# A two-layer hybrid trunk: shifted taps turned later, attention levels in pairs behind whole weight units, other places for the convolution's taps and placements

## The chip, the cores and the metric

The kernel runs on one core of one Trainium2 chip. The metric is the device time of one execution in microseconds (us); lower is better. The kernel before took 1219.56 us, the median of three runs (1218.1 to 1220.88).

## The reference

A decoder trunk over 256 tokens of width 1024, float32 in and out, two layers deep. The part that this change touches is the token mixer:

```python
z = h @ w_in                       # q, k, v, g, gr, ca, cb
gate_logit = gr @ w_gate_up + b_gate
log_a = log_sigmoid(gate_logit) / 16
o = gla_chunked(q * 64**-0.5, k, v, log_a)   # 4 heads, causal, decay exp(cumsum(log_a))
o = rmsnorm(o, gla_norm_w) * silu(g)
u = ca * sigmoid(cb)
u = causal_dwconv(u, conv_w, conv_b)         # 512 channels, 31 taps
u = silu(layernorm(u, cn_w, cn_b))
x = x + concatenate([o, u]) @ w_out
```

Behind the mixer of layer 0 stands a dense SwiGLU (width 2816), behind that of layer 1 a top-2-of-8 mixture of experts of the same width, and at the end an RMSNorm.

## The kernel before

**Weights.** Every weight matrix is cut into units of 128x2048 floats (1 MB). SyncE loads a unit into `raw` (11 slots); ScalarE (ACT) rounds it to a high part `w_hi` (`hi`, L610, 1.9 us); VectorE (DVE) makes the low part `w_lo` (`lo`, L1005, 2.3 us; `lo_half` is half of that). TensorE (PE) multiplies high by high, high by low and low by high. For an input unit these are 48 matmuls of 256 columns (L1728 to L1730 for activations in channel layout, L1762 to L1764 for token layout); `channels("CA1")` is a whole unit, `gates_tile(g, t)` and each half `f` of `channels_unit` are half a unit, 24 matmuls. `b` is the number of a layer's first unit; in layer 0 the units `b+3`, `b+4`, `b+5` are Q, K, V1.

**Attention.** The causal product is taken in nine levels (block sizes 128, 64, ... 1, and the diagonal). `level(n)` on PE (L1982) is a run of small float32 matmuls over 64 rows, 16 records in the trace (8 for level 0). Its input is made by `differences(n)` (DVE), `decays(n)` (ACT, exp) and `decayed(n)` (DVE, L1159, two buffers in turn), and its result is read by ACT for levels 0 to 2 and by `level_read_out(n)` on DVE (L1203) from level 3 on. Two pairs of PSUM banks take the levels in turn, so level n waits for the read-out of level n-2. Behind the levels come `heads()` (L1943 to L1945, the product with v), ACT's `head_squares`, DVE's `head_sums`, ACT's `head_roots`, DVE's `head_gates` (L1178), PE's `turn_heads` (L1955), ACT's `head_hi` (L718), DVE's `head_lo` (L1185).

**Convolution.** Of the four groups of 128 channels, group 0 is done on DVE, one instruction a tap, in two chains `acc` and `acc_odd` (L1123; `conv(k)` on DVE does the next k of 31 taps). Groups 1 to 3 are done on PE (`conv(k)` there, L1917, does the next k of 24 steps, 8 a group), on copies of the input that POOL's DMAs shift (`shifted`), with weights that DVE's `conv_weights` (L1070) expands from the taps `taps_x`. These taps come by DMA as rows in `shift_rows`, and PE turns them (`turn_params`, L2072) into PSUM, from where DVE copies them (L1210). When a group is done, `place(i)` on ACT (L728, four instructions) moves half of it with the bias to `acc`, and `add_ahead(i)` on DVE (L1091, four instructions) adds the other half. `sum_groups(0)` adds groups 0 and 1, and before that `acc_odd` to `acc` (L1103, L1106), `sum_groups(1)` groups 2 and 3. PE takes the layer norm's sums of these (L2052) inside the first output unit (`down_unit`, L1801, six pairs of 512-column matmuls, then the sums of `sum_groups(0)`, three pairs, the sums of `sum_groups(1)`, three pairs), DVE centres (L1349), ACT squares (L832), and PE sums the squares (L2060).

**Order.** Nothing is scheduled by a program. The order of the work on each engine is written out by hand in the function `mixer(l)` of each engine, once for `l == 0` and once for `l == 1` on DVE and ACT, and semaphores tie the engines together.

## Time and profile before

| | us |
|---|---|
| median of three runs | 1219.56 |
| lowest and highest run | 1218.1, 1220.88 |
| profiled execution | 1217.84 |
| its span in the trace | 1216.0 |
| PE busy in the span | 1197.2 |
| DVE busy | 967.0 |
| ACT busy | 783.8 |
| POOL busy | 93.7 |

The profiled execution lies 1.72 us below the median of the runs, and its span 1.84 us below its own time. Layer 0's mixer takes roughly the first 135 us of the span, the dense layer follows until about 320 us, layer 1's mixer until about 440 us, the experts take the rest. A busy PE is not a PE at its peak: each row of PE counts a matmul from issue to its modelled end, so ends overlap the next start. The pace is read from start to start.

### The profile page before, as it was taken

How to read it: one execution, taken by the hardware profiler on the slowest of the kernel's cores; microseconds unless marked ns; L12 is line 12 of the kernel's file. 1: busy time of each engine (PE TensorE's matmuls, PEld its weight loads, DVE VectorE, ACT ScalarE, POOL GpSimd, SP SyncE). 2: the span in 40 equal slices, each digit the busy share in tenths (PEclk: the TensorE clock that was granted, in tenths of full speed). 3: DMA queues.
4: the chain of work that ended last, by engine and by line, in shares of the span. 5: the costliest groups of instructions: out<-in, count | busy, mean ns of one | idle time of the engine just before them, and what ended most of it. 6: DMA issues, size and time to landing. Idle time of an engine off the chain costs nothing.

```text
span 1216.0 us, 16632 instructions
## 1 busy us (share of the span) xinstructions
PE 1197.2 (98%) x6712; PEld 1019.8 (84%) x6712; DVE 967.0 (80%) x890; ACT 783.8 (64%) x693; POOL 93.7 (8%) x160
## 2 busy tenths in 40 slices
PE   8999999999999999999999999999999999999997
PEld 7997999999899788888888888888888888888885
DVE  5988664445668879889979879879879879979987
ACT  5846544334564757677677768658658668767764
POOL 8220000000122000000000000000000000000000
PEclk9999999999999999999999999999999999999998
DMA  8972555655557259999999999999999999999980
GB/s 249 353 243 69 191 174 178 196 180 180 201 177 237 64 190 359 388 362 390 375 366 393 371 373 385 375 371 387 378 384 370 381 382 370 378 384 369 395 328 37
DMA packets 185003, 362.78 MB, mean 298 GB/s; under 512 B 10568, under 2 KB 70746, under 8 KB 184922
## 3 DMA queue, kind: packets, MB, share of 16 engines
q1 hardware_dynamic: 178170, 343.22, 79.3%
q0 software_dynamic: 6736, 18.43, 4.3%
q8 instruction: 56, 0.92, 0.3%
q14 instruction: 25, 0.20, 0.1%
q10 hardware_dynamic: 16, 0.00, 0.0%
HBM read 350.64 MB, written 7.86 MB: 295 GB/s over the span
## 4 chain that ended last, share of the span: by engine, by line
PE 93%; DVE 3%; ACT 2%; SPq 1%; issue 1%; DMA 0%; DVEq 0%; ACTq 0%
PE YB L2199 18%; PE WBS L2178 13%; PE WBS L2180 13%; PE WBS L2179 13%; PE YB L1801 5%; PE WBS L1728 5%; PE WBS L1730 4%; PE WBS L1729 4%; PE YB L2190 2%; PE YB L1782 2%; PE WBS L1762 2%; PE YB L2214 2%; PE WBS L1763 1%; PE WBS L1764 1%; PE YB L1982 1%
## 5 line engine op out<-in xcount | busy, mean ns | idle before, releaser
L1005 DVE TENSOR_TENSOR w_lo<-raw,w_hi 128x2048 fp32r<-128x2048 f32 x319 | 716.2, 2286 | 86.4 <-ACT w_hi L610 86.2
L610 ACT ACTIVATE w_hi<-raw 128x2048 fp32r<-128x2048 f32 x324 | 598.5, 1915 | 13.3 <-DMA raw<-in_w_in 8.1
L2178 PE MATMUL WBS<-w_hi,t_hi 128*128 128x512 f32 x704 | 279.2, 397 | 0.5 <-DVE w_lo L1005 0.5
L2180 PE MATMUL WBS<-w_hi,t_lo 128*128 128x512 f32 x704 | 275.0, 391 | 0.0
L2179 PE MATMUL WBS<-w_lo,t_hi 128*128 128x512 f32 x704 | 274.8, 390 | 0.0
L2178 PEld LDWEIGHTS WBS<-w_hi,t_hi 128*128 128x128 f32 x704 | 132.3, 188 | 29.1 <-issue 1.5
L2180 PEld LDWEIGHTS WBS<-w_hi,t_lo 128*128 128x128 f32 x704 | 132.3, 188 | 28.6
L2179 PEld LDWEIGHTS WBS<-w_lo,t_hi 128*128 128x128 f32 x704 | 132.5, 188 | 26.0
L1728 PE MATMUL WBS<-t_hi,w_lo 128*128 128x256 f32 x448 | 127.8, 285 | 0.0
L1729 PE MATMUL WBS<-t_hi,w_hi 128*128 128x256 f32 x448 | 126.9, 283 | 0.0
L1730 PE MATMUL WBS<-t_lo,w_hi 128*128 128x256 f32 x448 | 126.8, 283 | 0.0
L956 ACT ACTIVATE eT_hi<-YB 128x512 fp32r<-128x512 f32 (+1 forms) x48 | 27.0, 563 | 148.3 <-PE YB L2214 148.3
L2199 PE MATMUL YB<-w_hi,eT_hi 128*128 128x512 f32 x320 | 101.6, 399 | 0.3 <-DVE eT_lo L1652 0.3
L2199 PE MATMUL YB<-w_hi,eT_lo 128*128 128x512 f32 x320 | 100.7, 396 | 0.0
L2199 PE MATMUL YB<-w_lo,eT_hi 128*128 128x512 f32 x320 | 100.1, 394 | 0.0
L1728 PEld LDWEIGHTS WBS<-t_hi,w_lo 128*128 128x128 f32 x448 | 85.9, 192 | 1.5 <-issue 0.7
L1729 PEld LDWEIGHTS WBS<-t_hi,w_hi 128*128 128x128 f32 x448 | 86.0, 192 | 0.4
L1730 PEld LDWEIGHTS WBS<-t_lo,w_hi 128*128 128x128 f32 x448 | 86.0, 192 | 0.0
L2199 PEld LDWEIGHTS YB<-w_lo,eT_hi 128*128 128x128 f32 x320 | 60.1, 188 | 14.9
L2199 PEld LDWEIGHTS YB<-w_hi,eT_lo 128*128 128x128 f32 x320 | 60.1, 188 | 14.1
L2199 PEld LDWEIGHTS YB<-w_hi,eT_hi 128*128 128x128 f32 x320 | 59.4, 188 | 14.4 <-issue 0.7
L962 ACT ACTIVATE eg<-WBS 128x512 f32<-128x512 f32 (+1 forms) x48 | 26.9, 560 | 65.6 <-PE WBS L2180 65.6
(320 smaller groups left out, 1389.2 us busy)
## 6 DMA issues: line engine op xcount, KB each, us to landing
raw<-in_we_down SPq DMA_DIRECT2D x88, 1024.0 KB, 7.1
raw<-in_we_gate SPq DMA_DIRECT2D x80, 1024.0 KB, 6.8
raw<-in_we_up SPq DMA_DIRECT2D x80, 1024.0 KB, 6.6
raw<-in_w_in SPq DMA_DIRECT2D x19, 1024.0 KB, 6.5
raw<-in_wd_gate SPq DMA_DIRECT2D x11, 1024.0 KB, 5.4
raw<-in_wd_up SPq DMA_DIRECT2D x11, 1024.0 KB, 5.3
raw<-in_wd_down SPq DMA_DIRECT2D x11, 1024.0 KB, 5.0
raw<-in_w_out SPq DMA_DIRECT2D x8, 1024.0 KB, 9.5
```

Of the source, the lines that this page charges most:

```text
L610: act.activation(w_hi[:, hi_slot(n, item), :], raw[slot][:], ACT.Copy).then_inc(hi_ready, 1)
L956: act.activation(eT_hi[:, 0:w, :], YB[:, 3, 0:P * w].rearrange("p (f t) -> p f t", f=w), ACT.Copy).then_inc(eT_hi_ready, 1)
L962: act.activation(eg[:, 0:w], WB[c % 2][:, 0:w], ACT.Silu).then_inc(egate_ready, 1)
L1005: dve.tensor_tensor(w_lo[slot][:], raw[slot][:], w_hi[:, hi_slot(n, item), :].bitcast(F32), ALU.subtract).then_inc(lo_ready, 1)
L1728: pe.matmul(dst, lo[:, k, cols], t_hi[:, k, :], start=(k == 0), stop=False)
L1729: pe.matmul(dst, hi[:, k, cols], t_hi[:, k, :], start=False, stop=False)
L1730: ins = pe.matmul(dst, hi[:, k, cols], t_lo[:, k, :], start=False, stop=(k == KD - 1))
L1801: ins = pe.matmul(YB[:, 2 * t + half, :], a[:, k0 + k, tok], w[:, k, HALF * half:HALF * (half + 1)], start=(first and k == 0 and s), stop= ...
L2178: pe.matmul(bank, xs_hi[:, k0 + k, :], hi[:, k, :], start=start, stop=False)
L2179: pe.matmul(bank, xs_hi[:, k0 + k, :], lo[:, k, :], start=False, stop=False)
L2180: ins = pe.matmul(bank, xs_lo[:, k0 + k, :], hi[:, k, :], start=False, stop=stop)
L2199: ins = pe.matmul(YB[:, half, :], a[:, f, :], w[:, k, HALF * half:HALF * (half + 1)], start=(first and s), stop=(last and e))
```

## The change

- **The shifted taps.** `turn_params` no longer waits for `shift_rows` nor turns them. A new `turn_shift_rows` on PE turns them into PSUM bank YB 3 between the units CB0 and Q of layer 0; a new `shifted_taps` on DVE copies them to `taps_x` between `lo(b + 4)` and `conv_input(0)`; K, which is multiplied into the same bank, waits for that copy. `shift_rows` now lies in the memory of `acc_odd`, and its old place stays as filler. The buffer `idle` grows from 40 to 48 floats a partition, which moves all that is allocated behind it by 32 bytes.
- **The levels.** Before, levels 2 to 6 each stood behind or inside one half unit, and 7 and 8 together behind the last. After, levels 2 and 3 stand behind all of CA1, 4 and 5 behind both halves of G0, 6 and 7 behind both halves of G1; then come two steps of the convolution, level 8, and the other six of the group.
- **The placements.** On ACT `place(1)` moves ahead of `head_hi()`. On DVE `add_ahead(1)` moves ahead of the two `head_lo`.
- **DVE's taps.** In layer 0 seven are new behind `lo(b + 6)`, 12 instead of 14 stand ahead of `conv_input(1)`, four behind the `conv_weights` instead of three before them and one behind, none behind `head_gates` or `head_lo`. In layer 1 the 14 become 12, and five stand behind `head_lo` instead of two before and one behind. `level_read_out(7)` and `(8)` now stand ahead of the last two `conv_weights`.

```diff
@@ memory
-        idle = sb("idle", [P, 40])
+        idle = sb("idle", [P, 48])
-        shift_rows = sc("shift_rows", [P, L, P])
-        sc("beside_cu", [P, 2880 - L * P])
+        sc("beside_cu", [P, 2880])
         acc_odd = sm("acc_odd", [P, T])
+        shift_rows = acc_odd[:].rearrange("p (l c) -> p l c", l=L)
@@ ACT, mixer(l), both layers
                     head_roots()
+                    place(1)
                     head_hi()
-                    place(1)
                     place(2)
@@ DVE
+            def shifted_taps():
+
+                dve.wait_ge(shift_turned, 1)
+                dve.wait_ge(gr_done, 1)
+                dve.tensor_copy(taps_x.rearrange("p l q b -> p (l q b)"), YB[:, 3, 0:L * QS * 24]).then_inc(taps_x_ready, 1)
+
             def conv_weights(l, i):
 
                 if l == 0 and i == 0:
                     dve.wait_ge(ident4_ready, 1)
+                    dve.wait_ge(taps_x_ready, 1)
...
                 if l == 0:
-                    dve.wait_ge(turned_rows, 2 + L)
-                    dve.wait_ge(gr_done, 1)
-                    dve.tensor_copy(taps_x.rearrange("p l q b -> p (l q b)"), YB[:, 2, 0:L * QS * 24])
+                    dve.wait_ge(turned_rows, 2)
@@ DVE, mixer(0)
                     lo(b + 4)
+                    shifted_taps()
                     conv_input(0)
                     lo(b + 5)
                     conv(6)
                     lo(b + 6)
+                    conv(7)
                     decayed(0)
...
-                    conv(14)
+                    conv(12)
                     conv_input(1)
...
                     level_read_out(6)
-                    conv(3)
+                    level_read_out(7)
+                    level_read_out(8)
                     conv_weights(0, 1)
                     conv_weights(0, 2)
-                    level_read_out(7)
-                    level_read_out(8)
-                    conv(1)
+                    conv(4)
                     add_ahead(0)
                     head_sums(0)
                     head_sums(1)
                     head_gates()
-                    conv(2)
+                    add_ahead(1)
                     head_lo(0)
                     head_lo(1)
-                    conv(3)
-                    add_ahead(1)
                     sum_groups(0)
@@ DVE, mixer(1)
-                    conv(14)
+                    conv(12)
...
                     level_read_out(6)
+                    level_read_out(7)
+                    level_read_out(8)
                     conv_weights(1, 1)
                     conv_weights(1, 2)
-                    level_read_out(7)
-                    level_read_out(8)
                     add_ahead(0)
...
                     head_gates()
-                    conv(2)
+                    add_ahead(1)
                     head_lo(0)
                     head_lo(1)
-                    conv(1)
-                    add_ahead(1)
+                    conv(5)
                     sum_groups(0)
@@ PE, mixer(l)
                 if l == 0:
                     pe.wait_ge(params_ready, 1)
+                    turn_shift_rows()
                 channels("Q")
+                if l == 0:
+                    pe.wait_ge(taps_x_ready, 1)
                 channels("K")
...
-                channels("CA1", between=lambda: level(2))
-                channels("CB1", between=lambda: level(3))
+                channels("CA1")
+                level(2)
+                level(3)
+                channels("CB1")
                 gates_tile(0, 0)
+                gates_tile(0, 1)
                 level(4)
-                gates_tile(0, 1)
                 level(5)
                 gates_tile(1, 0)
+                gates_tile(1, 1)
                 level(6)
-                gates_tile(1, 1)
                 level(7)
+                conv(2)
                 level(8)
-                conv(8)
+                conv(6)
                 heads()
@@ PE, turn_params
-                pe.wait_ge(shift_rows_ready, 16 * L * QS * 2)
...
-                for rows, n in ((shift_rows[:, 0, :], 24 * QS), (shift_rows[:, 1, :], 24 * QS), (tap_rows[:], L * TAPS * 2), (pv_rows[:], L * NPV + KD)):
+                for rows, n in ((tap_rows[:], L * TAPS * 2), (pv_rows[:], L * NPV + KD)):
...
+            def turn_shift_rows():
+
+                pe.wait_ge(shift_rows_ready, 16 * L * QS * 2)
+                n = 24 * QS
+                for l in range(L):
+                    ins = pe.transpose(YB[:, 3, n * l:n * (l + 1)], shift_rows[0:n, l, :], ident[0:n, 0:n])
+                ins.then_inc(shift_turned, 1)
```

## Rows read from the trace of the kernel before

**Rows 1.** The page: the span, and the chain that ended last, by engine.
```profile
span 1216.0 us, 16632 instructions
...
PE 93%; DVE 3%; ACT 2%; SPq 1%; issue 1%; DMA 0%; DVEq 0%; ACTq 0%
```

**Rows 2.** Windows, the experts: stretch, length, busy PE, PEld, DVE, ACT, POOL, PEclk, DMA, GB/s.
```profile
470.00:1216.00 746.00, 736.69 (x3331) 602.60 (x3329) 648.52 (x473) 524.83 (x387) 26.92 (x19) 1.00 0.98 362
```

**Rows 3.** Timeline of PE, levels 4 and 5: start, duration (us), engine, line, operation.
```profile
71.31 1.11 PE L1982 MATMUL YB<-qkE 64*128 64x64 f32 x16
...
75.42 1.11 PE L1982 MATMUL YB<-lnw 64*128 64x64 f32 x16
```

**Rows 4.** Timeline of PE, end of G1, levels 7 and 8, the convolution before and after the heads.
```profile
83.30 0.28 PE L1763 MATMUL WBS<-w_lo,t_hi 128*128 128x256 f32 x1
83.42 0.28 PE L1764 MATMUL WBS<-w_hi,t_lo 128*128 128x256 f32 x1
83.63 1.11 PE L1982 MATMUL YB<-lnw 64*128 64x64 f32 x16
84.57 1.11 PE L1982 MATMUL YB<-qk 64*128 64x128 f32 x16
85.61 3.67 PE L1917 MATMUL WBS<-shifted,shift_w 128*64 128x256 f32 x32
...
92.09 4.97 PE L1917 MATMUL WBS<-shifted,t_mem 128*64 128x256 f32 x44
```

**Rows 5.** Timeline of PE, level 1 (behind level 0) and the first matmuls of CA1.
```profile
53.33 1.01 PE L1982 MATMUL YB<-lnw 64*128 64x64 f32 x16
54.27 0.39 PE L1728 MATMUL WBS<-t_hi,w_lo 128*128 128x256 f32 x1
54.49 0.28 PE L1729 MATMUL WBS<-t_hi,w_hi 128*128 128x256 f32 x1
```

**Rows 6.** Timeline of PE, the turned rows at the start, and the next matmul.
```profile
19.08 0.39 PE L2072 MATMUL YB<-ident,shift_rows 96*128 96x96 f32 x2 [2.81 <-DMA pv_rows<-in_ln_w]
19.30 0.27 PE L2072 MATMUL YB<-ident,tap_rows 124*128 124x124 f32 x1
```

**Rows 7.** Timeline of DVE, layer 0, two places ahead of the levels' products.
```profile
47.83 0.69 DVE L1159 TENSOR_TENSOR qkE<-qk,Difs 128x512 f32<-128x512 f32 x1 [2.81 <-ACT qk L693]
...
73.24 0.68 DVE L1159 TENSOR_TENSOR lnw<-qk,Difs 128x512 f32<-128x512 f32 x1
```

**Rows 8.** Timeline of PE, layer 0, the layer norm's sums inside the first output unit.
```profile
104.68 0.71 PE L2052 MATMUL WBS<-shifted,ones 128*128 128x128 f32 x4 [0.79 <-DVE shifted L1106]
...
106.88 0.71 PE L2052 MATMUL WBS<-shifted,ones 128*128 128x128 f32 x4
...
109.38 1.83 PE L2060 MATMUL WBS<-shifted,ones 128*128 128x128 f32 x14 [0.39 <-ACT shifted L832]
```

**Rows 9.** Timeline of DVE, layer 0, from behind the last `head_lo` to the half unit ahead of the centring.
```profile
100.70 0.47 DVE L1123 SCALAR_TENSOR_TENSOR acc<-cu,taps,acc 128x256 f32<-128x256 f32 x1
101.09 0.48 DVE L1123 SCALAR_TENSOR_TENSOR acc_odd<-cu,taps,acc_odd 128x256 f32<-128x256 f32 x1
...
102.00 1.71 DVE L1091 TENSOR_TENSOR acc<-acc,WBS 32x240 f32<-32x240 f32 x4
...
106.74 1.22 DVE L1012 TENSOR_TENSOR w_lo<-raw,w_hi 128x1024 fp32r<-128x1024 f32 x1
```

**Rows 10.** Timeline of ACT, layer 0: `head_hi`, then `place(1)` and `place(2)`.
```profile
98.66 1.27 ACT L718 ACTIVATE t_hi<-WBS,pv 128x512 fp32r<-128x512 f32 x2 [3.62 <-PE WBS L1955]
99.81 3.89 ACT L728 ACTIVATE acc<-WBS,pv 32x256 f32<-32x256 f32 x8
```

**Rows 11.** Timeline, layer 1: DVE's `sum_groups(0)`, PE's sums and sums of squares.
```profile
409.25 0.43 DVE L1106 TENSOR_TENSOR shifted<-acc 128x256 f32<-128x256 f32 x1
...
409.74 0.71 PE L2052 MATMUL WBS<-shifted,ones 128*128 128x128 f32 x4
...
414.43 1.83 PE L2060 MATMUL WBS<-shifted,ones 128*128 128x128 f32 x14 [0.39 <-ACT shifted L832]
```

More of the change, by code:

```diff
@@ L271, in trunk @@
         cgate_ready, cu_ready, pads_ready = (sem(s) for s in ("cgate_ready", "cu_ready", "pads_ready"))
+        shift_turned, taps_x_ready = sem("shift_turned"), sem("taps_x_ready")
         shift_rows_ready, shift_pads, conv_grouped, odd_added = (sem(s) for s in (
@@ L479, in _ @@
             step(pool.memset(ones[:], 1.0))
-            step(pool.memset(shift_rows[:], 0.0))
+            step(pool.memset(shift_rows, 0.0))
             for l in range(L):
@@ L823, in mixer @@
                     head_roots()
+                    place(1)
                     head_hi()
-                    place(1)
                     place(2)
@@ L1207, in mixer @@
                 if l == 0:
-                    dve.wait_ge(turned_rows, 2 + L)
-                    dve.wait_ge(gr_done, 1)
-                    dve.tensor_copy(taps_x.rearrange("p l q b -> p (l q b)"), YB[:, 2, 0:L * QS * 24])
-                    taps_at = L * QS * 24
-                    pv_at = taps_at + L * TAPS * 2
-                    dve.tensor_copy(taps[:].rearrange("p l w c -> p (l w c)"), YB[:, 2, taps_at:pv_at])
+                    dve.wait_ge(turned_rows, 2)
+                    pv_at = L * TAPS * 2
+                    dve.tensor_copy(taps[:].rearrange("p l w c -> p (l w c)"), YB[:, 2, 0:pv_at])
                     dve.tensor_reduce(ident4[:], ident[:].rearrange("p (s j) -> p j s", s=4), AX, ALU.add).then_inc(ident4_ready, 1)
```

## The prediction

> **What bounds the kernel now.** I read the page first. The span is 1216.0 us and PE carries 93% of the chain that ended last [rows 1]. So only what shortens PE's stream, or takes a wait out of it, moves the end. Then the windows: among the experts PE is busy 736.69 of 746 us at the full granted clock, 1.00, that is its level of 2.4 GHz, and no other engine sits above 87% [rows 2]. SyncE loads and ACT rounds when PE frees a slot, so that stage starts earlier by whatever the mixers save and keeps its length. Then the timeline of PE through both mixers, for two things: what each switch between kinds of matmul costs, and where PE stands idle. It issues without a gap from the turned parameters on until the first convolution group, and the real idle time lies at the layer norm's sums (0.79 and 0.39 us in layer 0, 0.39 in layer 1 [rows 8, 11]). Last the timelines of DVE and ACT, for what ends these waits, and for whether the inputs of the levels come in time for the new order.
>
> **Levels in pairs: price of a switch.** Weight matmuls start 0.12 us apart, and the first record of level 7 starts 0.21 behind the last of them, so 0.09 is lost on entry [rows 4]. On the way out 0.22 lies between the first and the second weight matmul, so 0.10 is lost there [rows 5]. A level with another level on one side of it, 7 ahead of 8 and 1 behind 0, takes 0.94 from its start to the next one's [rows 4, 5]. For a lone one I take the distance of levels 4 and 5, 4.11 us, less 24 x 0.12 = 2.88 for the half unit between: 1.23 with its switches [rows 3]. A pair costs 0.09 + 0.94 + 0.94 + 0.10 = 2.07, against 2.46 for two lone ones.
> Before, a layer has five lone levels (2 to 6), 6.15, and 7 with 8 from the end of G1 to the convolution, 85.61 - 83.42 - 0.12 = 2.07 [rows 4]: 8.22. After: two pairs 4.14; 6 with 7, entry 0.09, 0.94, 0.94, and up to 0.10 at the exit, 2.02 in the middle; then level 8, 1.04 as it stands before the convolution now [rows 4]; and one switch more, from the convolution back to a level. Nothing in the trace shows that direction. Its nearest rows are the exit of 8 to the convolution (1.04 against 0.94, so 0.10) and the entries above; I take 0.10 and allow 0 to 0.3. Sum 7.30, gain 0.92 a layer, with bounds 0.7 and 1.07. Both layers: -1.84, bounds -1.4 and -2.14.
> The Trainium skill (TensorEngine Tiling (Array Packing), Key Properties) says that a change of tiling mode, though not of the tile, drains TensorE. Levels are 64*128 and the convolution is 128*64, so by that rule splitting 7, 8, convolution into 7, convolution, 8, convolution adds two drains. The rows give such a drain about 0.1 us, which is already in the sum; it would have to be 0.5 each to eat a layer's gain.
>
> **The shifted taps.** At the start two turned rows leave PE's stream; both start within 0.22 us [rows 6], -0.22. The wait of 2.81 us ahead of them stays, since it ends with `pv_rows`, not with `shift_rows` [rows 6]. Between CB0 and Q the same 0.22 comes back with an entry and an exit, 0.09 + 0.10: +0.41 at most, and 0.22 at least. Net +0.15, bounds 0 and +0.2. The turned rows' wait for the DMA is long past by then, since they were turned at 19 us already. DVE's copy moves from its idle start to before `conv_input(0)`; DVE is then ahead: seven new taps and the copy go into a slot in which DVE waited 2.81 us for ACT's q and k [rows 7]. Seven taps at 0.39 us (100.70 to 101.09 [rows 9]) are 2.7, the copy about 0.3, so `decayed(0)` starts some 0.3 later than 47.83; PE comes to level 1 only at 53.33 [rows 5], so this costs nothing. Queued behind DVE's wait and copy stand `conv_input(0)` and V1's low part, which PE wants only after the whole of Q and K (2 x 48 x 0.12 = 11.5 us). K on PE waits for the copy; it waits for K's low part anyway, which DVE makes just before, and it comes a whole unit (5.8 us) behind the turned rows. Taken at nothing; if DVE came later than that, each microsecond would be PE's.
> The DMA issues do not move. The memory of `acc_odd` is free until the first tap. The 32 bytes of `idle` shift the address of tiles behind it; the product into `qkE` (behind) and into `lnw` (ahead) take 0.69 and 0.68 [rows 7], so place does not show. Taken at 0.
>
> **The tail of layer 0.** This is the larger part of its kind. Between the last `head_lo` and `sum_groups(0)` DVE now does three taps (100.70 to 102.00) and `add_ahead(1)`, 1.71 [rows 9]; both go, to idle slots: the taps to earlier places, `add_ahead(1)` into the time in which PE turns the heads and ACT makes `head_hi`. For that ACT must have done `place(1)` ahead of `head_hi`: it takes half of 3.89, 1.95 [rows 10], and ACT waited 3.62 before `head_hi` [rows 10]. So acc_sum(0) comes 1.30 + 1.71 = 3.0 us earlier, against PE's wait of 0.79 [rows 8]: the wait goes, and PE's own stream is next. The second sums: `add_ahead(2)` then hangs on `place(2)`, which cannot start before PE's last group is done, at the start of the output unit; place 1.95, one last quarter of 1.71 (0.43) and a sum of 0.43 [rows 9 to 11] put acc_sum(1) about 2.8 us behind that start. PE wants it behind six pairs of wide matmuls and then 2.20 later (104.68 to 106.88 [rows 8]), some 5 us behind. No wait. Third, the wait of 0.39 for the squares [rows 8]: the half unit of weights on DVE, 1.22, ran until 107.96 and held up the centring although PE's sums had begun at 106.88 [rows 8, 9]. It now runs well ahead of them, and the centring starts some 0.4 to 0.5 earlier, so this wait goes too. -0.79 - 0.39 = -1.18; small waits without a mark of their own ahead of the second sums (the trace leaves 0.1 to 0.2 there) make it -1.3. Bounds -0.8 and -1.5.
>
> **The tail of layer 1.** Here five taps stand behind `head_lo`, 2.0 us, where one tap and `add_ahead(1)` stood, 0.39 + 1.71 = 2.1. So acc_sum(0) comes 0.1 earlier. It was ready at 409.68 and PE took it at 409.74 without a marked wait [rows 11], so nothing to win there. The wait of 0.39 [rows 11] hangs on the same half unit on DVE, which again runs right ahead of the centring: it stays nearly whole. -0.2, bounds 0 and -0.4.
>
> **Sum.** -1.84 + 0.15 - 1.3 - 0.2 = -3.2. Against the profiled execution, 1217.84, that is 1214.6; the median lies 1.72 above it, so 1219.56 - 3.2 = 1216.4. From the bounds: -1.4 + 0.2 - 0.8 - 0 = -2.0, and -2.14 + 0 - 1.5 - 0.4 = -4.0, so 1215.5 to 1217.6. What a measurement of this kernel can tell from no change is about 0.2%, 2.4 us: below 1217.1 is faster, above 1222.0 slower.
>
> **Rivals.** (1) The tail of layer 0 gives nothing back. `place(1)` now stands ahead of `head_hi` on ACT, and can't begin before PE has done group 1. Group 0 ended at 89.28, the second convolution stretch starts at 92.09, and a group takes 3.6 [rows 4]: group 1 is done 6.4 us after group 0, place(1) at 8.4, and `head_hi` was released at 98.66, 9.4 after it [rows 10]: about 1.0 of slack. For it: group 1's weights are made later on DVE, behind two read-outs. Against it: they are ready about 2 us before PE wants them. If the slack is missed by about 1.3 a layer, the tails are lost, and the switches remain: 1219.56 - 1.7 = 1217.9, no change that can be told. (2) The change doesn't do what it says: the switches cost the same in pairs, because what a lone level loses is lost at each level's start. Against it: level 8 follows level 7, and level 1 follows level 0, at 0.94 or less [rows 4, 5]. Then only the tails count: 1219.56 - 1.35 = 1218.2. (3) Slower: the second level of a pair wants its input 0.94 us after the first, where it had 4.11 [rows 3]. The mechanism is level 5. Its product on DVE ran at 73.24 [rows 7], behind CB1's gate, a table load on ACT and the low part of a unit, none of which comes sooner after CB1; PE now wants it at about 74.9: level 4 from 71.31 [rows 3] half a unit (2.88) back, 0.39 forward for the pair ahead, 0.15 back for the taps, and 0.94 for level 4 itself. The product ended at 73.92, slack 1.0. Levels 7 and 8 have the same form with slacks of 1 to 3 us. From a lateness of 1.0 on PE stalls; at 2.6 the layer's gain of 1.6 is eaten, and the kernel is measurably slower once both layers are late by about 3.8. With 4.2 each it would be 1219.56 - 3.2 + 2 x 3.2 = 1222.8.
>
> **How the numbers follow.** The forecast gets 0.64, rival 1 0.17, rival 2 0.08, rival 3 0.05, and 0.06 for mixtures near zero. Of the forecast's own cases a small part falls above 1217.1, and some of the rivals' falls below it. Faster by over 0.2%: 0.64; within 0.2%: 0.31; slower by over 0.2%: 0.05. The time is that of the likeliest, 1216.4. The range takes the bounds, 1215.5 to 1217.6, the spread of a median (the three runs differ by 2.8), and reaches to rivals 1 and 2: 1214.4 to 1218.9.
>
> **What would show it.** In the trace after: levels 2 and 3, 4 and 5, 6 and 7 start 0.94 apart, and from the last weight matmul of CA1 to the second one of CB1 there are about 2.3 us; level 8 stands 0.9 to 1.1 behind the first convolution steps and doesn't wait. From the start of the first output unit to the sums of squares it is 8.5 us in layer 0; now 7.1. No idle mark at L2052, none or a few hundredths at L2060 in layer 0, about 0.3 to 0.4 at L2060 in layer 1. ACT's L728 has four instructions ahead of L718. The prediction is wrong if PE waits for `qkE` or for `att` at a level, if `head_hi` starts later after the heads' transposes than now, or if the dense layer or the experts get longer: they should not change.

## The result, and the profile after

The changed kernel takes 1210.7 us, the median of four runs (1209.27 to 1211.27), against 1220.15 for the kernel before, run beside it (four runs, 1218.1 to 1220.88). The ratio is 0.9923, with a 95% interval of 0.9906 to 0.9941: it is 9.4 us faster, where 3.2 was forecast and the range went down to 1214.4. The profiled execution took 1211.27, its span 1209.4. The page of after answers to [rows 1]:

```profile
span 1209.4 us, 16633 instructions
...
PE 93%; DVE 3%; ACT 1%; SPq 1%; issue 1%; DMA 0%; ACTq 0%; DVEq 0%
```

PE still carries 93% of the chain, so the gain must be found in PE's own stream. I cut the span at starts of PE that every kernel has: level 0 of layer 0, the transposes behind layer 0's mixer (seam 1), those ahead of layer 1's (seam 2), the layer norm's sums in layer 1. Each entry is the difference of two starts in the timeline of PE (us).

| stretch | before | after | difference |
|---|---|---|---|
| start to level 0 | 52.78 | 54.51 | +1.73 |
| level 0 to seam 1 (mixer of layer 0) | 73.91 | 71.25 | -2.66 |
| seam 1 to seam 2 (dense layer) | 190.85 | 189.99 | -0.86 |
| seam 2 to the sums of layer 1 | 92.20 | 91.37 | -0.83 |
| those sums to the end (the experts, mostly) | 806.26 | 802.28 | -3.98 |

The mixers give 3.5, which is the forecast's 3.2 in its place. The dense layer and the experts, which "should not change", give 4.8. The first stretch went the other way in this execution, mostly by TensorE's clock; it is taken up at the end.

First the mixers. The timeline of PE in after, at the end of layer 0's levels (start, duration, engine, line, operation), answers to [rows 4]:

```profile
83.46 1.11 PE L1985 MATMUL YB<-qkE 64*128 64x64 f32 x16
84.41 1.06 PE L1985 MATMUL YB<-lnw 64*128 64x64 f32 x16
85.39 1.08 PE L1920 MATMUL WBS<-shifted,shift_w 128*64 128x256 f32 x8
86.41 1.16 PE L1985 MATMUL YB<-qk 64*128 64x128 f32 x16
87.50 2.81 PE L1920 MATMUL WBS<-shifted,shift_w 128*64 128x256 f32 x24
90.24 0.49 PE L1946 MATMUL WBS<-v,att 128*128 128x128 f32 x2
```

The last row is the first of `heads()`. Levels 6 and 7 stand 0.95 apart, level 8 follows 1.02 behind the start of conv(2), and nothing waits. Then layer 0's tail, PE first, which answers to [rows 8]:

```profile
101.98 0.70 PE L1804 MATMUL YB<-w_hi,t_hi 128*128 128x512 f32 x2
...
104.79 0.60 PE L2061 MATMUL WBS<-shifted,ones 128*128 128x128 f32 x4
...
106.61 0.60 PE L2061 MATMUL WBS<-shifted,ones 128*128 128x128 f32 x4
...
108.44 1.27 PE L2069 MATMUL WBS<-shifted,ones 128*128 128x128 f32 x9
```

None of the three has an idle mark. On DVE the two summed groups end well ahead of PE's two sums, and the half unit of weights is done before the centring, where it held it up before [rows 9]:

```profile
102.25 0.42 DVE L1114 TENSOR_TENSOR shifted<-acc 128x256 f32<-128x256 f32 x1
...
104.49 0.42 DVE L1114 TENSOR_TENSOR shifted<-acc 128x256 f32<-128x256 f32 x1
104.83 1.22 DVE L1013 TENSOR_TENSOR w_lo<-raw,w_hi 128x1024 fp32r<-128x1024 f32 x1
107.03 1.29 DVE L1352 SCALAR_TENSOR_TENSOR acc<-WBS,acc 128x512 f32<-128x512 f32 x2 [0.98 <-PE WBS L2061]
```

In layer 1 one wait stays, as in [rows 11]:

```profile
411.82 1.05 PE L2069 MATMUL WBS<-shifted,ones 128*128 128x128 f32 x7 [0.39 <-ACT shifted L833]
```

Now the place where 4.0 us came from. The groups of PE's matmuls by line among the experts, from 470 to 1190 us (line, engine, operation, count, busy us, mean ns, idle). Before:

```profile
L2178 PE MATMUL WBS<-w_hi,t_hi 128*128 128x512 f32 x666 | 264.0, 396 | 0.0
L2180 PE MATMUL WBS<-w_hi,t_lo 128*128 128x512 f32 x665 | 259.8, 391 | 0.0
L2179 PE MATMUL WBS<-w_lo,t_hi 128*128 128x512 f32 x665 | 259.6, 390 | 0.0
L2199 PE MATMUL YB<-w_hi,eT_hi 128*128 128x512 f32 x311 | 98.8, 399 | 0.3 <-DVE eT_lo L1652 0.3
L2199 PE MATMUL YB<-w_hi,eT_lo 128*128 128x512 f32 x312 | 98.2, 396 | 0.0
L2199 PE MATMUL YB<-w_lo,eT_hi 128*128 128x512 f32 x312 | 97.6, 394 | 0.0
```

After:

```profile
L2194 PE MATMUL WBS<-w_hi,t_hi 128*128 128x512 f32 x672 | 266.2, 396 | 0.0
...
L2215 PE MATMUL YB<-w_hi,eT_hi 128*128 128x512 f32 x310 | 97.2, 395 | 0.3 <-DVE eT_lo L1655 0.3
L2215 PE MATMUL YB<-w_lo,eT_hi 128*128 128x512 f32 x309 | 95.6, 390 | 0.0
L2215 PE MATMUL YB<-w_hi,eT_lo 128*128 128x512 f32 x308 | 95.5, 391 | 0.0
```

The first line is the gate and up projections: 396 ns in both. The down projection's matmuls read the turned activations `eT_hi` and `eT_lo` as their stationary operand (the one that is loaded into TensorE ahead of the matmul), and those of L2199 take 4 to 5 ns less. The count is large: 132 in one expert, 1056 in eight (960 of them on L2199), and 264 with `dT` in the dense layer. From start to start the 960 give 4.13 us, 4.3 ns each; what makes 3.98 of it is taken apart behind e6. Nobody edited these lines. What did change for them is where their tiles start: `idle`, 32 bytes longer, lies ahead of `dT` and `eT`, and behind `t_hi`, `w_hi` and the `w_lo` of the units. In the program as built `dT_hi` starts at byte 184096 of its partition before, which is 32 past a multiple of 64 (and of 128), and at 184128 after, a multiple of 64 (64 past one of 128); `eT_hi` has the same remainders.

### The profile page after: what moved, and what is told of

Its sections match the earlier page's. It is cut to its first block, busy times and chain, and to the rows that moved or that the text cites. A ratio compares the mean times of both kernels' runs of the same rounds, so it can differ in the third digit from the quotient of the medians.

```text
span 1209.4 us, 16633 instructions
## 1 busy us (share of the span) xinstructions
PE 1191.6 (99%) x6712; PEld 1020.5 (84%) x6712; DVE 966.9 (80%) x890; ACT 784.1 (65%) x693; POOL 93.9 (8%) x160
## 4 chain that ended last, share of the span: by engine, by line
PE 93%; DVE 3%; ACT 1%; SPq 1%; issue 1%; DMA 0%; ACTq 0%; DVEq 0%
PE YB L2215 18%; PE WBS L2194 13%; PE WBS L2196 13%; PE WBS L2195 13%; PE YB L1804 5%; PE WBS L1731 5%; PE WBS L1733 4%; PE WBS L1732 4%; PE YB L2206 2%; PE WBS L1765 2%; PE YB L2230 2%; PE WBS L1767 2%; PE WBS L1766 2%; PE YB L1985 1%; PE YB L1785 1%; PE YB L1731 1%
```

## Experiments on the place of the tiles

Theory A: the 32 bytes make the down projections faster, through the start of `dT` and `eT`, and the reordering gives what was forecast. Rival: the time in the later stages comes from the reordering (slots that come free at other times), and the 32 bytes do nothing.

**e1_idle48: the 32 bytes alone.**

```diff
-        idle = sb("idle", [P, 40])
+        idle = sb("idle", [P, 48])
```

> The kernel before with one edit: idle 48 instead of 40 floats a partition, so every tile allocated behind it lies 32 bytes further (dT_hi at byte 184128 of a partition instead of 184096, a multiple of 64 instead of 32 beyond one). Theory A, the address: matmuls whose stationary operand lies behind idle (dT, eT) start about 4.5 ns closer, nine to ten ns a pair; the dense layer's down units go from 5.60 to 5.50 us, the experts get some 4 us shorter, together 4.8 us: about 1215.4. Theory B, the address does nothing and the 4 us in the experts come from how the changed program lies or from what the mixers leave behind: 1220, the down units stay at 5.60.

Measured: 1212.91 (5 runs, 1212.71 to 1214.12) against 1219.36, ratio 0.9954 [0.994, 0.9967]. Its dense layer takes 189.98 and its last stretch 802.34, as in after; its mixers take what they took before (73.92 and 92.19). By these stretches that is 4.8 us, so one number of `idle` gives more than all the reordering. The medians say 6.4, and 1212.91 lies below the 1215.4 that was expected. Three of e1's five runs have a mean granted clock of 0.998, where none of the 21 beside it is above 0.997; what that does to a run's time is in the last section.

**e2_after_idle40: the kernel after without the 32 bytes.**

```diff
-        idle = sb("idle", [P, 48])
+        idle = sb("idle", [P, 40])
```

> The changed kernel with idle back at 40 floats: all of the reordering, none of the shift. Theory A: down units back at 5.60 us, experts as long as before, only the mixers' 3.4 us remain: about 1216.8. Theory B: as the changed kernel, 1210.7.

Measured: 1215.89 (11 runs, 1214.28 to 1217.61), ratio 0.9971 [0.9962, 0.998], so 3.5 us faster than before. Mixer of layer 0 71.25 as in after, dense layer 190.87 and last stretch 806.3 as before. The two halves of the change add, and this half lies within the forecast's bounds of 2.0 to 4.0.

**e3_turned_only: only `dT` and `eT` moved.** `idle` stays at 40; eight floats of filler stand ahead of `dT_hi` and of `eT_hi`, and another eight behind `eT_lo`. The tiles behind those, `sel` and `selT` among them, lie 64 bytes further.

```diff
         dact = sd("dact", [P, 512])
+        sd("beside_dT", [P, 8])
         dT_hi = sd("dT_hi", [P, 2, 2, T], F32R)
...
         eact = se("eact", [P, 512])
+        se("beside_eT", [P, 8])
         eT_hi = se("eT_hi", [P, 4, P], F32R)
         eT_lo = se("eT_lo", [P, 4, P], F32R)
+        se("behind_eT", [P, 8])
```

> The kernel before, idle at 40, with a filler of 8 floats ahead of dT_hi, one ahead of eT_hi and one behind eT_lo: only the turned activations of the dense layer and of the experts (the stationary operands of the down matmuls) move by 32 bytes; everything else behind idle keeps its place modulo 64. Theory A in its narrow form, the stationary operand's address alone: the whole 4.8 us, 1215.4. In its wide form (writes by ACT and DVE, DMAs, other tiles): a part of it or nothing, 1217 to 1220. Theory B: 1220.

Measured: 1213.31 (1211.81 to 1215.12), ratio 0.9954 [0.994, 0.9967], the same as e1's within the scatter; dense layer 189.96, last stretch 801.24. So moving these four tiles gives the whole of it, and the tiles of the mixer, of `dg` and `dact`, and of the experts ahead of `eT_hi` don't have to move. The last stretch is even 1.1 shorter than e1's, mostly in gate and up matmuls (table behind e6).

**e4_idle56, e5_idle72, e6_idle64: other distances.** One line each, `idle` 56, 72 and 64 wide: 64, 128 and 96 bytes instead of 32.

> The kernel before with idle at 56 floats: the tiles behind move by 64 bytes, so again 32 beyond a multiple of 64. If what counts is the place modulo 64: as before, 1220, down units 5.60. If any move helps, or what counts is modulo 128 with 96 better than 32: faster, 5.50.

> The kernel before with `idle` 72 wide instead of 40: everything behind it lies 128 bytes further, so the tiles stand to a 128-byte grid as before. Theory A (the 32 bytes act through the address of the experts' and the dense layer's stationary operands to a grid of 64 bytes, with a small second effect of the distance 64): as before, 1218.5 to 1220.5, down units of 24 matmuls at 5.60 us, one expert 94.5 to 94.6 in the trace. Rival B (any other place of these tiles is better than the one of before, for instance because of what it lies beside): 1213 to 1217, with down units at 5.50. If it comes out at 1217.4 like the run with 64 bytes, the small second gain there has nothing to do with the 64 bytes themselves.

> The kernel before with `idle` 64 wide instead of 40: 96 bytes, so 32 past the 64-byte grid of before as with 8 floats, but on the other side of a 128-byte grid. Theory A: the down units take 5.50 us instead of 5.60, time 1212 to 1214; if the small gain of the run with 64 bytes adds to it, 1211 to 1212. Rival B (a grid of 128 bytes counts, and only +32 meets it): as before, 1218.5 to 1220.5.

The first line of 24 down matmuls in a row (two units of weights; called a down unit here) and the first line of what follows them, from the timeline of PE in the same expert. Before, then after, then e4_idle56, e3_turned_only and e6_idle64:

```profile
658.74 0.63 PE L2199 MATMUL YB<-w_hi,eT_hi 128*128 128x512 f32 x2
...
664.34 0.40 PE L2178 MATMUL WBS<-w_hi,t_hi 128*128 128x512 f32 x1
```

```profile
655.16 0.62 PE L2215 MATMUL YB<-w_hi,eT_hi 128*128 128x512 f32 x2
...
660.66 0.39 PE L2194 MATMUL WBS<-w_hi,t_hi 128*128 128x512 f32 x1
```

```profile
660.90 0.63 PE L2199 MATMUL YB<-w_hi,eT_hi 128*128 128x512 f32 x2
...
666.49 0.39 PE L2178 MATMUL WBS<-w_hi,t_hi 128*128 128x512 f32 x1
```

```profile
657.98 0.62 PE L2202 MATMUL YB<-w_hi,eT_hi 128*128 128x512 f32 x2
...
663.47 0.39 PE L2181 MATMUL WBS<-w_hi,t_hi 128*128 128x512 f32 x1
```

```profile
657.19 0.61 PE L2199 MATMUL YB<-w_hi,eT_hi 128*128 128x512 f32 x2
...
662.63 0.39 PE L2178 MATMUL WBS<-w_hi,t_hi 128*128 128x512 f32 x1
```

Start to start that is 5.60, 5.50, 5.59, 5.49 and 5.44. All of the runs with one number of `idle` changed, by where `dT` and `eT` start (us; an expert is the distance of two expert starts on PE; "beside" is the kernel before in the same comparison):

| `idle` | start past a multiple of 128 | down unit | one expert | time | beside |
|---|---|---|---|---|---|
| 40 (before) | 32 | 5.60 | 94.59 | | |
| 48 (e1) | 64 | 5.50 | 94.12 | 1212.91 | 1219.36 |
| 56 (e4) | 96 | 5.59 | 94.38 | 1217.37 | 1219.36 |
| 64 (e6) | 0 | 5.44 | 93.84 | 1211.22 | 1219.63 |
| 72 (e5) | 32 | 5.60 | 94.40 | 1217.47 | 1219.63 |

A start off the 64-byte grid costs 0.10 us in 24 matmuls against 64 past a multiple of 128, and a start on a multiple of 128 saves 0.06 more. For that reason e6 (ratio 0.9927 [0.9912, 0.9942]) came out at the better of its two expectations (1211 to 1212), though that one had put the gain down to something else. There is a remainder that theory A did not expect. e4 and e5 keep the slow down unit, yet an expert takes 0.2 less than before, and both kernels are 2 us faster (ratios 0.9981 [0.9971, 0.999] and 0.9979 [0.997, 0.9989]); e5 was expected at 1218.5 to 1220.5 and missed. In the timeline the 24 gate or up matmuls right behind a down unit take 5.45 instead of 5.49 in e4, e5 and e6, in e1 and e3 too. Summed from start to start over the last stretch (us):

| | before | e5 | after | e3 |
|---|---|---|---|---|
| 960 down matmuls, L2199 | 224.71 | 224.58 | 220.58 | 220.64 |
| 96 down matmuls, the last unit of each expert, L2190 | 22.81 | 22.94 | 23.28 | 23.20 |
| 672 gate and up matmuls right behind L2199 | 153.69 | 152.65 | 152.65 | 152.48 |
| the other 1440 gate and up matmuls | 333.31 | 332.98 | 334.03 | 333.11 |
| all else | 71.76 | 71.63 | 71.77 | 71.78 |

(The lines are those of before.) So the 3.98 is a balance. The start on the 64-byte grid is the difference of after and e5, 2.5 us: 4.0 less on L2199, but 0.3 more on L2190 and 1.1 more in other gate and up matmuls. Of that last loss 0.9 is absent in e3, so it comes with tiles behind `idle` that e3 left in place; which ones is open. The other 1.5 us of the 3.98 comes with any of the new places. What makes it is open: every kernel with `dT` and `eT` at the start of before has the 5.49 (before, e2, e7, e8, e10), and no other one has it.

**Smaller distances: e12, e16, e13, e14, e15.** `idle` 44, 42, 52, 60 and 68 wide, one line each, to tell a grid of 64 from a distance to it.

> The kernel before with `idle` 44 wide instead of 40: everything behind it 16 bytes further, 48 past a multiple of 64. Theory A1 (what costs is any start off the 64-byte grid, because a row of the stationary tile then lies across one line more): down units 5.60 us as before, 1217.3 to 1219.8. Rival A2 (the cost grows with the distance to the grid, 16 bytes being half as bad as 32): down units near 5.55, 1215 to 1217. Rival A3 (16-byte offsets are worse than 32): down units above 5.62 and a time above 1221.

> The kernel before with `idle` 42 wide: 8 bytes further, dT and eT 40 past a multiple of 64. Theory P (the remainder counts in steps of 16 bytes, 32 to 47 being the costly one): 5.60, one expert 94.4 to 94.6. Rival (only exactly 32 is costly): 5.50, 94.1. Rival (starts off a 16-byte step cost more than any other): above 5.60.

> The kernel before with `idle` 52 wide: tiles behind it 48 bytes further, dT and eT 80 past a multiple of 128. Theory P (what counts is the remainder to 64, and the costly ones lie at 32 only): down units 5.50 us, one expert about 94.1. Theory Q (the row of a stationary operand, 512 bytes, is worst when it starts at or behind 32 and below 48 past a multiple of 64): 5.50 too. Theory R (it isn't the remainder at all but the mere place of before): 5.50 to 5.60, not told by it.

> The kernel before with `idle` 60 wide: 80 bytes further, dT and eT 112 past a multiple of 128, 48 past one of 64. Theory P: 5.50 as with `idle` 44, whose remainder to 64 is the same. If a grid of 128 counts and 112 differs from 48, a value between 5.44 and 5.60 that differs from 5.50 by more than 0.02.

> The kernel before with `idle` 68 wide: 112 bytes further, dT and eT 16 past a multiple of 128. Theory P (only remainder 32 to 64 is costly): 5.44 to 5.50, one expert 93.85 to 94.1. Rival (what matters is a multiple of 128 exactly, and the first 16 bytes off it cost as much as the next): 5.50 or above.

Measured: 1213.42 (e12, 4 runs, beside 1219.61, ratio 0.9954 [0.9939, 0.9969]), and in one execution each, beside 1220.45, 1214.12 (e16), 1217.73 (e13), 1211.22 (e14) and 1217.66 (e15); experts 94.12, 94.12, 94.40, 93.84 and 94.40. The expectations missed in several places (e12's 1213.4 fits none of its three theories, and theory P had an expert of e15 near 93.85 to 94.1). The reason is in the program, not in the chip: as built, `dT_hi` starts at 184128 in e12 and e16, at 184160 in e13, 184192 in e14 and 184224 in e15. Tiles are placed in steps of 32 bytes, so these five have the starts of e1, e1, e4, e6 and e5. They are repeats and give the same experts to within 0.02. A start between two steps was not tried by any run.

## Experiments on the reordering

**e7_levels_only: PE's new order of levels alone.**

```diff
-                channels("CA1", between=lambda: level(2))
-                channels("CB1", between=lambda: level(3))
+                channels("CA1")
+                level(2)
+                level(3)
+                channels("CB1")
...
+                conv(2)
                 level(8)
-                conv(8)
+                conv(6)
```

> The kernel before with PE's new order of levels alone (levels 2 with 3, 4 with 5, 6 with 7 behind whole units, conv(2), level 8, conv(6)); `idle` stays at 40, and DVE's and ACT's orders and the shifted taps stay as before. The prediction's step: 0.92 us a layer, so -1.84 with bounds -1.4 and -2.14: 1217.2 to 1218.0 against 1219.4, and in the trace 36.4 us from level 0 to the heads' transposes falls to 35.5 in each layer. Rival (the switches cost the same in pairs): 36.4 stays and the time is 1219.0 to 1219.8. Rival (the second level of a pair waits for its product when DVE keeps its old order): idle marks at levels 3, 5 or 7 and less than 0.9 a layer.

Measured: 1219.41 (11 runs) against 1219.63, ratio 0.9997 [0.9988, 1.0006]: nothing. What the expectations call the heads' transposes is the first row of `heads()`, L1943, a product with v. Level 0 to that row takes 37.43 in layer 0 and 36.33 in layer 1, not 35.5. PE's timeline has a wait in layer 0, and DVE's shows what stood in the way; `<-issue` names nothing, but `heads` needs the read-outs of levels 7 and 8 in `att`:

```profile
92.13 0.46 PE L1943 MATMUL WBS<-v,att 128*128 128x128 f32 x2 [1.63 <-issue]
```

```profile
87.07 2.35 DVE L1070 TENSOR_TENSOR t_mem<-ident,gr_mem 128x1024 f32<-128x1024 f32 x2
89.34 2.68 DVE L1203 COPY_PREDICATED att<-masks,YB 128x512 f32<-128x512 uint8 x2
```

The read-outs end at 92.02, and `heads` starts at 92.13. They queue behind three taps and two `conv_weights`, 2.35 us. In layer 1 the same wait is 0.53. Without its wait the stretch would be 37.43 - 1.63 = 35.80 in layer 0, and 36.33 - 0.53 = 35.80 in layer 1, 0.64 less than before in each.

**e10_levels_readouts: e7, and on DVE the read-outs of 7 and 8 moved ahead of these taps and weights.** The same move is made in layer 1.

```diff
                     level_read_out(6)
+                    level_read_out(7)
+                    level_read_out(8)
                     conv(3)
                     conv_weights(0, 1)
                     conv_weights(0, 2)
-                    level_read_out(7)
-                    level_read_out(8)
```

> The kernel with the levels' new order alone, and on DVE the read-outs of levels 7 and 8 moved ahead of the taps and the weights of groups 1 and 2 that stood before them; `idle` 40. Theory A (with the levels alone PE waits 1.63 us in layer 0 and 0.53 in layer 1 for `att` ahead of the heads' transposes, because these read-outs queue behind 2.35 us of conv_weights and three taps; moving them gives it back): no idle ahead of the heads' transposes, 35.7 us from level 0 to them in both layers, time 1217.6 to 1218.6. Rival (group 1's weights then come late, and PE waits at the second group of the convolution instead): 35.7 as well, but an idle mark or a longer stretch between the heads' transposes and their turning, and 1219 to 1219.8.

Measured: 1218.32 (11 runs) against 1219.61, ratio 0.9992 [0.9983, 1.0001]. No wait, 35.73 in layer 0 and 35.74 in layer 1, where both had 36.44. The last read-out now stands at 87.58, 2.6 us ahead of `heads` at 90.20:

```profile
84.58 2.72 DVE L1203 COPY_PREDICATED att<-masks,YB 128x512 f32<-128x512 uint8 x2 [2.52 <-PE YB L1982]
87.58 1.31 DVE L1203 COPY_PREDICATED att<-masks,YB 128x1024 f32<-128x1024 uint8 x1 [0.28 <-PE YB L1982]
```

By the traces the two mixers give 0.63 and 0.73. The interval of the time just reaches 1, so the time alone doesn't show the gain; the step is carried by the traces, which agree on 0.70 to 0.71 in both layers of e10, e2, e9 and after.

**e8_orders_only: everything but the levels.** The kernel after with `idle` 40, one level behind each half unit, 7 and 8 together, and `conv(8)`.

```diff
-                channels("CA1")
-                level(2)
-                level(3)
-                channels("CB1")
+                channels("CA1", between=lambda: level(2))
+                channels("CB1", between=lambda: level(3))
...
                 level(7)
-                conv(2)
                 level(8)
-                conv(6)
+                conv(8)
```

> The kernel after with `idle` back at 40 and PE's levels as before (one behind each half unit, 7 and 8 together, conv(8)); the later shifted taps, the taps' and the placements' new order stay. The prediction's step: +0.15 for the shifted taps, -1.3 for the tail of layer 0, -0.2 for that of layer 1, together -1.35: 1217.7 to 1218.6 against 1219.4. In the trace from the first output unit to the sums of squares 6.5 to 7.1 us in layer 0 instead of 8.5, and from level 0 to the heads' transposes 36.4 in both layers as before. Rival (the tail's gain comes only together with the new order of the levels): 8.5 stays, 1219.0 to 1219.8. The four edits' parts should then add: this run and the one with the levels alone together give the 3.5 of the kernel after with `idle` at 40.

Measured: 1217.51 (11 runs) against 1219.63, ratio 0.9983 [0.9974, 0.9992], 2.1 us faster. That is just below the 1217.7 to 1218.6 expected. First output unit to the sums of squares 6.50 in layer 0 (103.63 to 110.13), no wait among the sums; level 0 to `heads` 36.43; layer 1 changes by 0.08. So the tail's gain needs nothing of the levels, and e8 and e10 together, 2.1 and 1.3, make the 3.5 of e2.

**e9_after_idle64: the kernel after, `idle` 64 wide.**

```diff
-        idle = sb("idle", [P, 48])
+        idle = sb("idle", [P, 64])
```

> The kernel after with `idle` 64 wide instead of 48, so everything behind it lies on a grid of 128 bytes and not only of 64. Theory A (the address of dT and eT sets how fast TensorE goes through the down units: 5.60 us for 24 at 32 or 96 past a multiple of 128, 5.50 at 64, 5.44 at 0; and it adds to what the reordering gives): 1219.5 - 8.4 - 3.5 = 1207.6, within 1207.0 to 1209.3, one expert 93.85. Rival (the reordering and the addresses aren't additive, and the kernel after stands at its best): 1210 to 1212.

Measured: 1206.2 (4 runs, 1206.14 to 1209.34) against 1219.61, ratio 0.9889 [0.9874, 0.9904]. Dense layer 189.68, last stretch 800.04, mixers as in after. It beats both kernels. Against after the medians differ by 4.5 us, these stretches by 2.6; the expectation was 1207.0 to 1209.3, so the median lies below it, with three runs at 1206.1 to 1206.2 and one at 1209.34.

**e11_unsplit: e9 with level 8 right behind level 7.**

```diff
                 level(7)
-                conv(2)
                 level(8)
-                conv(6)
+                conv(8)
```

> The kernel after with `idle` 64, level 8 right behind level 7 and conv(8) unsplit behind both. The split costs by the trace 1.02 + 1.09 + 2.74 = 4.85 where level 8 and conv(8) together should take 0.94 + 0.10 + 3.6 = 4.6: theory A: 0.2 to 0.25 less a layer, -0.4 to -0.5 against the run with `idle` 64 of the same call, 35.5 from level 0 to the heads' transposes. Rival (the split is there so that the read-out of level 7 has time; without it the read-outs or group 1's weights come late): an idle mark ahead of the heads' transposes or ahead of the second group, and no less or more time than with the split.

Measured: 1208.63 (5 runs, 1207.06 to 1209.92), ratio 0.9912 [0.9899, 0.9926], no better than e9. From level 0 to `heads` it takes 36.15 in layer 0 and 36.16 in layer 1, 0.42 more than with the split, and PE now waits:

```profile
81.97 1.06 PE L1985 MATMUL YB<-lnw 64*128 64x64 f32 x16
83.54 1.16 PE L1985 MATMUL YB<-qk 64*128 64x128 f32 x16 [0.51 <-DVE att L1211]
```

```profile
82.19 4.12 DVE L1211 COPY_PREDICATED att<-masks,YB 128x512 f32<-128x512 uint8 x3 [2.51 <-PE YB L1985]
```

Three read-outs of 1.3 us stand in a row on DVE, and level 8 needs the bank pair that level 6 filled. conv(2) between 7 and 8 covers that read-out. My sum had the split only as a cost. The trace gives 0.84 for both layers; the rest of the 2.4 between the two medians is not explained by it and lies within the scatter described last (e11's lowest run, 1207.06, is below e9's highest).

## Why the prediction was wrong

**The step that failed** is the last sentence on `idle`: the 32 bytes "shift the address of tiles behind it; the product into `qkE` (behind) and into `lnw` (ahead) take 0.69 and 0.68 [rows 7], so place does not show. Taken at 0." These rows are two operations on DVE. They say nothing on what PE reads, and of the tiles behind `idle` the ones with the most uses are stationary operands of 1320 matmuls. The trace of before had the sign of it: among matmuls of one shape in one stage, the down projection's high by high took 399 ns where the gate's took 396, and 396 and 394 where those took 391 and 390. I didn't read these groups, since "the dense layer or the experts" weren't edited. The price is 4.8 us by the table (0.86 + 3.98) and by e1's stretches, and it is why the time fell outside the range. Of these, 0.86 and 2.5 go with the start against the 64-byte grid; for the other 1.5 the runs show that it comes with the move, and not why. As "what would make it wrong" the text named only that those stages get longer.

**What PE's clock adds to the comparison.** The medians differ by 9.4, the spans by 6.6. The stretch up to level 0 was 1.73 longer in after's profiled execution, 1.5 of it by a fall of the clock (last section), the rest because PE got its rows 0.2 later. 6.6 + 1.7 = 8.3 is the gain without it; the lowest runs, 1209.27 and the 1217.85 of before, differ by 8.6. The table's stretches behind level 0 are the firmest measure, 3.5 + 4.8.

**Levels in pairs: right in kind, 0.71 a layer instead of 0.92.** It is at the lower bound of 0.7. Levels 4 and 6 stand 7.88 apart (75.54 to 83.42 in e10), less 48 x 0.12 = 5.76 a pair costs 2.12, not 2.07. Level 8 takes 1.09, not 1.04, and conv(2) and conv(6) take 1.02 + 2.74 = 3.76 where conv(8) took 3.61 [rows 4], 0.15 for the switch from convolution to level instead of 0.10. On the drain of the Trainium skill (TensorEngine Tiling (Array Packing), Key Properties) the trace agrees in kind: each change of mode costs 0.09 to 0.15 here, and it didn't eat the gain. That it is a drain that costs this, no run shows.

**What the sum had at nothing: the read-outs.** The move of read-outs 7 and 8 ahead of `conv_weights` has no term; rival 1 names it, as a cost alone. e7 against e10 prices it: in e7 DVE reads level 6, which comes later now, at 84.81, then does the taps and weights, and reads level 7 only at 89.34, with level 8 done at 92.02 where PE would go on at 90.5. PE waits 1.63 and 0.53. The text said that the prediction is wrong if PE waits for `att` at a level; the change had taken care of it, and I had not seen that it was needed.

**Shifted taps: within its bounds of 0 and 0.2, but about 0 and not 0.15.** In after's timeline of PE, between CB0 and Q:

```profile
36.83 0.28 PE L1733 MATMUL WBS<-t_lo,w_hi 128*128 128x256 f32 x1
36.95 0.33 PE L2088 MATMUL YB<-ident,acc_odd 96*128 96x96 f32 x2
37.06 0.36 PE L1731 MATMUL YB<-t_hi,w_lo 128*128 128x256 f32 x1
37.27 0.28 PE L1732 MATMUL YB<-t_hi,w_hi 128*128 128x256 f32 x1
```

From 36.83 to 37.27 is 0.44, where two weight matmuls take 0.24: +0.20, less than the 0.37 in the sum (0.15 + 0.22). At the start the turned rows take 0.43 instead of 0.60, -0.17 and not -0.22. From the end of the wait for `pv_rows` to level 0 it takes 33.70 in before (19.08 to 52.78) and in e2 (19.67 to 53.37). No wait of K for the copy.

**Tail of layer 0: right in kind, 2.03 instead of 1.3**, outside its bound of 1.5. From the output unit to the squares it is 6.46 where 8.49 stood; 7.1 was expected. The marked waits, 0.79 and 0.39 [rows 8], are shorter than the holes in the starts. These are the last pairs of wide matmuls ahead of the three, from the timeline of PE in before:

```profile
103.27 0.61 PE L1801 MATMUL YB<-w_hi,t_lo 128*128 128x512 f32 x2
...
106.16 0.63 PE L1801 MATMUL YB<-w_hi,t_lo 128*128 128x512 f32 x2
...
108.36 0.63 PE L1801 MATMUL YB<-w_hi,t_lo 128*128 128x512 f32 x2
```

Pairs are 0.46 apart, so the hole ahead of the first sums was 104.68 - 103.27 - 0.46 = 0.95. The second sums, with no mark, had one of 0.26, and the squares one of 0.56. Behind each wait the four sums took 0.47 instead of 0.36, 0.11 more. Together 0.95 + 0.26 + 0.56 + 0.22 = 1.99. The term for "small waits without a mark" was 0.1 where 0.8 was right. Another wait of layer 0 has no place in the prediction and stays: ahead of the heads' turning (L1955) PE waits 0.47 for DVE's `qk` in before and 0.54 in after.

**Tail of layer 1: right.** 0.08 by e8, within 0 to 0.4, and the wait of 0.39 stays.

**The rivals.** None of the three happened. Rival 1 (tail of layer 0 gives nothing) falls by the tail: ACT, with `place(1)` done, still waits 0.98 for PE ahead of `head_hi`, about the slack of 1.0 that the rival gave it. Rival 2 (switches cost the same) falls by the levels' rows; rival 3, level 5 waiting for its product, shows no mark in any run. What did come too late in the variants was DVE's read-out behind a level, not its product ahead of one: at `heads` (e7) and at level 8 (e11).

## What to carry to other kernels

When an edit changes the size of any tile, write down which tiles lie behind it and which of them TensorE reads most often; their rows, and not those of another engine, say what a place is worth, and some 4 ns in most of 1320 matmuls outweighed all hand-made reordering here. Then add up the whole stretch, since other matmuls moved too, some of them the other way. To look for it in a profile, compare the mean of matmuls of one shape across lines; a difference of 1% between two lines that do the same work is a lead. Measure a wait from start to start of the neighbours, because the idle marks of layer 0's tail show 1.18 of 1.99 us. Where units on one engine are regrouped, follow each partner's read-out on the other engine to the next user.

## What the runs showed of the hardware

**Where a stationary operand starts matters to TensorE.** A stationary operand of 128 columns of four bytes that started 32 or 96 bytes past a multiple of 128 gave 5.60 us for 24 matmuls of 512 columns; 64 past it 5.50; on it 5.44. The difference is 4 and 2.5 ns a matmul. The dense layer goes the same way (190.9, 190.0, 189.7 us). It isn't so of every matmul that reads these tiles: the 12 of an expert's last unit (L2190), which take one half of the output after the other, took 2.80 us, 2.87 and 2.89. The profile's own time of a load of these operands is 188 ns at 32, at 64 and at 0 alike. The reason inside the chip was not measured. Only one type and one shape was tried, and the weights, which these matmuls read as the other operand, lie ahead of `idle` and never moved.

**The clock behind the wait for `pv_rows`.** PE waits 2.3 to 3.0 us at 16 to 20 us in every kernel (2.81 in before, 2.83 in after). In some executions the granted clock falls from 1.00, the level of 2.4 GHz, to 0.50, that of 1.2 GHz, about when the work goes on. The windows from 18 to 24 us (stretch, length, busy PE, PEld, DVE, ACT, POOL, clock, DMA, GB/s), of before, of after and of e9_after_idle64:

```profile
18.00:24.00 6.00, 4.92 (x40) 4.74 (x41) 2.15 (x7) 1.28 (x1) 3.72 (x8) 1.00 1.00 302
```

```profile
18.00:24.00 6.00, 4.72 (x25) 4.56 (x26) 1.87 (x6) 0.85 (x1) 3.70 (x8) 0.72 1.00 286
```

```profile
18.00:24.00 6.00, 5.09 (x23) 4.81 (x24) 1.65 (x6) 1.23 (x1) 3.85 (x9) 0.52 1.01 300
```

In after's timeline of PE the weight matmuls start 0.12 apart, then 0.21, and 0.12 again from 23.81 on:

```profile
20.17 0.28 PE L1765 MATMUL WBS<-w_hi,t_hi 128*128 128x256 f32 x1
20.29 0.30 PE L1766 MATMUL WBS<-w_lo,t_hi 128*128 128x256 f32 x1
...
21.25 0.41 PE L1765 MATMUL WBS<-w_hi,t_hi 128*128 128x256 f32 x1
21.46 0.41 PE L1766 MATMUL WBS<-w_lo,t_hi 128*128 128x256 f32 x1
...
23.81 0.30 PE L1765 MATMUL WBS<-w_hi,t_hi 128*128 128x256 f32 x1
```

From 20.41 to 23.81 there are 16 matmuls, which at 0.12 would take 1.9 us, so it costs 1.5. In e4, e8 and e9 the clock is low for longer, from about 18.5 to 25 us: from the first weight matmul of this stretch to level 0 it takes 35.4 to 35.8, where before takes 33.1 at the full clock. Over the executions profiled, level 0 starts between 52.1 and 55.5 us, 3.4 apart, which is about the spread of one kernel's runs (before: 1217.85 to 1221.22). Within one kernel the mean granted clock of a run goes with its time: of the 21 runs of before beside e1, three have 0.997 and took 1217.85 to 1218.08, twelve 0.996 and 1219.11 to 1219.99, six 0.995 and 1220.24 to 1221.22. That is why medians here scatter by a microsecond or two with few runs, and why small steps were read from the stretches behind level 0. Where in those runs the clock was low is not on record; that this fall makes up the whole of the spread is an inference.
